# Up tiles of the experts in transfers of 2 MB, and transposes of the identity on TensorE while the experts' places are worked out

## The reference

```python
def moe_ffn(h, router_w, w1, w3, w2):
    logits = (h @ router_w).astype(jnp.float32)
    top_vals, top_idx = lax.top_k(logits, TOP_K)
    ...
    for e in range(N_EXPERTS):
        out = out + gate[..., e:e + 1].astype(h.dtype) * swiglu(h, w1[e], w3[e], w2[e])
    return out

def swiglu(h, w1, w3, w2):
    return (jax.nn.silu(h @ w1) * (h @ w3)) @ w2
```

## Time and profile before

| | |
|---|---|
| median of 3 executions | 2174.63 us (2174.55 to 2176.81) |
| the profiled execution | 2175.69 us, its span 2173.9 us |
| TensorE busy | 2070.3 us (95%) |
| VectorE busy | 1270.5 us (58%) |
| ScalarE busy | 946.6 us (44%) |
| read from HBM | 485.91 MB |
| DMA queue of SyncE | 484.39 MB |

### The profile page before, as it was taken

How to read it: one execution, slowest core, us unless ns; L and a number is a source line. 1 busy time by engine, 2 the same in 40 slices (tenths; PEclk the granted TensorE clock), 3 DMA queues, 4 the chain that set the end, 5 groups by cost and what they waited for, 6 DMA issues and landing times. The chain is left out here.

```text
span 2173.9 us, 38831 instructions
## 1 busy us (share of the span) xinstructions
PE 2070.3 (95%) x15492; PEld 1737.7 (80%) x15492; DVE 1270.5 (58%) x2412; ACT 946.6 (44%) x1724; POOL 124.9 (6%) x115
## 2 busy tenths in 40 slices
PE   8999999999999999998999899998999999999997
PEld 7988888998978988888999888888556765568553
DVE  5465667565667776778665775777114931178211
ACT  5545544545554453446443544444014630065111
POOL 0100000010000024021000005012000000000000
PEclk9999999999999999999999999999999999999999
DMA  6443334444337444346554444339999999999997
GB/s 198 151 136 101 98 98 140 145 144 136 113 123 163 142 152 131 106 137 219 172 191 137 138 147 145 107 118 346 392 421 420 421 413 420 420 421 407 409 420 310
DMA packets 257818, 489.49 MB, mean 225 GB/s; under 512 B 35256, under 2 KB 208216, under 8 KB 223720
## 3 DMA queue, kind: packets, MB, share of 16 engines
q1 hardware_dynamic: 252112, 484.39, 61.6%
q0 software_dynamic: 656, 1.80, 0.2%
q10 hardware_dynamic: 4872, 0.81, 0.2%
HBM read 485.91 MB, written 1.05 MB: 224 GB/s over the span
## 5 line engine op out<-in xcount | busy, mean ns | idle before, releaser
L1356 PE MATMUL bank<-memr 128*128 128x256 f32 (+3 forms) x7056 | 896.6, 286 | 28.4 <-DVE memr L2417 9.7
L1356 PEld LDWEIGHTS bank<-memr 128*128 128x128 f32 (+2 forms) x7056 | 855.5, 185 | 58.8 <-issue 16.3
L2417 DVE TENSOR_TENSOR memr<-mem_low,memr 128x1024 fp32r<-128x1024 f32 (+3 forms) x328 | 400.0, 1238 | 63.8 <-ACT memr L1864 63.1
L1864 ACT CAST memr<-mem_low 128x1024 fp32r<-128x1024 f32 (+3 forms) x328 | 333.3, 1032 | 112.7 <-PE bank L1356 109.8
L1252 DVE SCALAR_TENSOR_TENSOR mem_high<-mem_high,bank 128x128 f32<-128x128 f32 (+1 forms) x88 | 28.0, 318 | 273.4 <-ACT mem_high L1053 273.4
L1053 ACT ACTIVATE mem_high<-bank 128x128 f32<-128x128 f32 (+1 forms) x88 | 26.7, 304 | 348.1 <-PE bank L869 322.8
L869 PE MATMUL bank<-mem_tail,mem_low 128*64 128x256 f32 x1088 | 127.5, 387 | 2.9 <-DMA mem_tail<-in_moe 2.3
L869 PEld LDWEIGHTS bank<-mem_tail,mem_low 128*64 128x64 f32 x1088 | 77.9, 139 | 54.2 <-issue 17.3
L660 PE MATMUL bank<-memr 128*128 128x256 f32 x960 | 115.6, 281 | 3.1 <-DVE memr L2436 3.1
L869 PE MATMUL bank<-mem_ring,mem_low 128*64 128x256 f32 x992 | 113.7, 381 | 3.7 <-DMA mem_ring<-in_moe 3.7
L660 PEld LDWEIGHTS bank<-memr 128*128 128x128 f32 x960 | 114.3, 189 | 3.5 <-issue 3.5
(11 more groups left out here) (367 smaller groups left out, 2815.6 us busy)
## 6 DMA issues: line engine op xcount, KB each, us to landing
mem_tail<-in_moe SPq DMA_DIRECT2D x132, 1024.0 KB, 15.4
mem_ring<-in_moe SPq DMA_DIRECT2D x128, 1024.0 KB, 16.2
mem_low<-in_w_in SPq DMA_DIRECT2D x112, 1024.0 KB, 5.2
mem_tail<-in_ffn_w SPq DMA_DIRECT2D x18, 1024.0 KB, 8.6
mem_low<-in_w_out SPq DMA_DIRECT2D x16, 1024.0 KB, 5.3
mem_low<-in_w_branch SPq DMA_DIRECT2D x12, 1024.0 KB, 5.0
mem_high<-in_ffn_w SPq DMA_DIRECT2D x12, 1024.0 KB, 8.1
mem_low<-in_w_branch SPq DMA_DIRECT2D x16, 512.0 KB, 3.5
```

What stands on the lines that cost most here:

```text
L1356: ins = pe.matmul(out(bank), lhsT, rhs, start=((k, i) == order[0] and not half), stop=((k, i) == order[-1]), skip_group_check=half is not ...
L1864: cp(high, raw).then_inc(*sig("w_high", i))
L2417: st(V.tensor_tensor(low, raw, high, ALU.subtract), sig("w_split", i))
```

## The change

Each chunk's two up tiles become one tile of 2 MB: the weights lie in memory so that a partition's 4096 numbers are contiguous, and one transfer brings them (128 rows of 16 KB in place of 128 rows of 8 KB twice). Of the twelve places eight become four pairs, used by up tiles alone, and four stay single, used by down tiles alone. Of the four places that are free after `chosen`, three and the fourth make room for the pairs of chunks 4 and 5; the second of these is still two transfers. A pair is asked for when both halves of the chunk four before it are finished, a down tile when the down tile four before it is. `LOAD_ORDER` keeps the order of use, but puts the pairs of chunks 4 and 5 after the tiles that can be loaded before `chosen`. On TensorE `keep_clock` transposes the identity matrix 12 times into the bank of the places before the wait for `chosen`, and 8 times into the bank `XB` behind the counts of places.

```diff
+PAIRS = 4
+RAW = 3 * PAIRS
+LOAD_ORDER = [n for n in range(TILES) if TILE_ORDER[n][1] != 1]
+LOAD_ORDER.sort(key=lambda n: (FIRST if PAIRS <= TILE_ORDER[n][0] < PAIRS + HI // 2 and TILE_ORDER[n][1] == 0 else n, n))
...
+        def pair_of(g):
+
+            return g if g < PAIRS + HI // 2 else (g - PAIRS - HI // 2) % PAIRS
...
+            def keep_clock(bank, n):
+
+                for _ in range(n):
+                    pe.transpose(bank[:, 0:P], const("ident"), const("ident"))
...
             ins.then_inc(*sig("token_sums", 0))
             tokens(1)
+            bank = open_group(("place",))
+            keep_clock(bank, 12)
 
             pe.wait_ge(*at("chosen"))
             pe.sem_inc(family("m_done"), HI)
...
             ins.then_inc(*sig(f"acc_full{unit['place',] % 2}", "place"))
+            keep_clock(XB, 8)
             pe.wait_ge(*evacuated("place"))
...
-                for n in range(TILES):
+                for n in LOAD_ORDER:
...
-                    if n < FIRST:
-                        sp.wait_ge(family("m_done"), p * (TILES + FIRST) + n + 1)
+                    k = pair_of(g)
+                    if j == 2 and g >= PAIRS:
+                        sp.wait_ge(*tile_done(p, down_tile(g - PAIRS)))
+                    elif j < 2 and g >= PAIRS + HI // 2:
+                        sp.wait_ge(*tile_done(p, up_tile(max(q for q in range(g) if pair_of(q) == k), 1)))
                     else:
-                        sp.wait_ge(*tile_done(p, n - (FIRST if n < FIRST + RAW else RAW)))
-                    src = a["moe"][bass.DynSlice(expert[i], 1), c, j].rearrange("o p f -> (o p) f") if i else a["moe"][0, c, j]
-                    sp.dma_start(raw[slot_of(n)], src).then_inc(raw_loaded(p, n)[0], 16)
+                        sp.wait_ge(family("m_done"), p * (TILES + FIRST) + (FIRST if j < 2 and k >= PAIRS else RAW))
+                    if j == 2:
+                        sp.dma_start(single[g % PAIRS], weights(expert, i, c, 2)).then_inc(raw_loaded(p, n)[0], 16)
+                    elif k > PAIRS:
+                        for half in range(2):
+                            sp.dma_start(last_raw[half], weights(expert, i, c, 0)[:, 2048 * half:2048 * (half + 1)])\
+                                .then_inc(raw_loaded(p, n)[0], 16)
+                    else:
+                        sp.dma_start(wide_hi[:, 0:4096] if k == PAIRS else pair[k], weights(expert, i, c, 0))\
+                            .then_inc(raw_loaded(p, n)[0], 16)
```

More of the change, by code:

```diff
@@ L44 @@
 W2B = 384
-RAW = 12
+PAIRS = 4
+RAW = 3 * PAIRS
 HI = 4
@@ L315, in build @@
         top[0] = upper
-        raw, raw_r = map(list, zip(*[carve_both(2048) for _ in range(6)]))
+        pair, pair_r = map(list, zip(*[carve_both(4096) for _ in range(3)]))
         top[0] = mark
-        for i in range(5):
-            raw.append(mem_ring[:, 2048 * i:2048 * (i + 1)])
-            raw_r.append(carve_both(2048)[1])
+        pair.append(mem_ring[:, 0:4096])
+        pair_r.append(carve_both(4096)[1])
+        single, single_r = [], []
+        for i in range(2, 5):
+            single.append(mem_ring[:, 2048 * i:2048 * (i + 1)])
+            single_r.append(carve_both(2048)[1])
         htok = [carve(D)]
@@ L758, in heavy_before, with raw_tile, raw_tile_r @@
             return sum(heavy(k) for k in range(i))
-        def slot_of(n):
-            return n if n < FIRST else (n - FIRST) % RAW
-        def raw_loaded(p, n):
[L766 to L772, removed]
+        def pair_of(g):
+            return g if g < PAIRS + HI // 2 else (g - PAIRS - HI // 2) % PAIRS
+        def raw_tile(n, singles=single, pairs=pair, rest=(wide_hi[:, 0:4096], last_raw)):
+            g, j = TILE_ORDER[n]
+            if j == 2:
+                return singles[g % PAIRS]
+            k = pair_of(g)
+            if k > PAIRS:
+                return rest[1][j]
+            return (rest[0] if k == PAIRS else pairs[k])[:, 2048 * j:2048 * (j + 1)]
+        def raw_tile_r(n):
+            return raw_tile(n, single_r, pair_r)
+        def raw_loaded(p, n):
+            g, j = TILE_ORDER[n]
+            if j == 2:
+                return family(f"m_down{g % PAIRS}"), 16 * (p * UPS // PAIRS + g // PAIRS + 1)
+            k = pair_of(g)
+            if k >= PAIRS:
+                last = max(range(k - PAIRS, len(chunks), NSLOT))
+                s, before = at(f"w_loaded{k - PAIRS}", last)
+                return s, before + 16 * (k - PAIRS + 1) * (p + 1)
+            of_place = [q for q in range(UPS) if pair_of(q) == k]
+            return family(f"m_up{k}"), 16 * (p * len(of_place) + of_place.index(g) + 1)
         def split_done(p, n):
@@ L857, in up @@
                         pe.wait_ge(*split_done(p, n))
-                        high, low = hi_r[SPLIT.index(n) % HI], raw_r[slot_of(n)]
+                        high, low = hi_r[SPLIT.index(n) % HI], raw_tile_r(n)
                         for k in range(4):
@@ L977, in moe_sync, with weights @@
         def moe_sync(sp):
+            def weights(expert, i, c, j):
+                lo, f = (0, 4096) if j < 2 else (P * 4096, 2048)
+                if i == 0:
+                    return a["moe"][0, c, lo:lo + P * f].rearrange("(p f) -> p f", f=f)
+                return a["moe"][bass.DynSlice(expert[i], 1), c, lo:lo + P * f].rearrange("o (p f) -> (o p) f", f=f)
             def body(p, learn):
                 expert = {0: 0}
-                for n in range(TILES):
+                for n in LOAD_ORDER:
                     g, j = TILE_ORDER[n]
```

33 lines of the change are left out of this document (17 added, 16 removed).

## The result

| | before | after |
|---|---|---|
| median, taken in turns on one chip | 2175.34 us (8 runs, 2172.32 to 2179.02) | 2182.88 us (8 runs, 2180.89 to 2187.78) |
| the profiled execution, its span | 2175.69, 2173.9 | 2183.04, 2181.1 |
| first transfer of the stage to its last landing | 672.9 | 679.3 |

The changed kernel is slower: the ratio is 1.0037, with a 95% interval of 1.0026 to 1.0047. Of the 7.2 us between the two spans the stage itself (first issue of `in_moe` to the last landing) has 6.4.

The account below looks back on a forecast made before the run. DMA at 420 GB/s was taken to bound light experts, TensorE heavy ones. Losses in the opening and at both heavy experts, less saved packets, summed to +7.6 us on the profiled 2175.69; median 2182, range 2174 to 2189.

Parts of the forecast that it names:

- Packets: Experts' stage: each pair loaded by one transfer saves 71 ns; 4.1 us (58 pairs) reach the end.
- 16 KB rows give nothing but marks: Rival, whole stage: 58 pairs lose 63 ns each of the saving, 3.7 us more, 2185.9 us; chance 0.1.
- the saving arrives whole: Rival, heavy stretches: the queue is not starved there, so the sum is -5.0 us, 2169.6; chance 0.1.
- Transposes: Before and through the gather: the 20 transposes hold TensorE's clock at 2.4 GHz, costing TensorE about 0.1 us.
- second rival: Opening: the transposes do not hold the clock, the sum is +13.1 us, 2187.7; chance 0.12.
- Opening: Start of the stage: a wait in SyncE's order loses 5.1 us where 3.9 was lost before, +1.2.
- First heavy start: First heavy expert: waiting for both halves puts its start at +2.1 us; a clock fall costs 2.5, TensorE leaves at +4.6.
- Second heavy start: Second heavy expert: its first chunk waits for a whole pair (+2.5 us), so TensorE starts at +7.0.
- The ends of the heavy experts: Low transfer rates there lose 7 to 8 us at each, where 0.5 and 2.6 were lost before.
- late asking: Heavy ends: a pair is asked for only when its second half is free; 1.2 us at the first, 1.8 at the second.
- the wait for a whole pair: Both heavy starts: both halves must have landed before work begins, 2.5 us later at each.
- The clock: First heavy expert: after a longer idle time TensorE's clock falls to 0.50, charged 2.5 us; no new price at the second.

Follow-up runs that it names:

- e: The changed kernel with each pair except chunk 4's brought by two 1 MB transfers, asked for together and counted on one semaphore; 2184.27 us.
- a: The changed kernel without its 20 transposes of the identity; 2186.52 us.
- c: The changed kernel with the pairs of chunks 7 and 8 ahead of the down tiles of chunks 4 and 5 in SyncE's order; 2180.62 us.
- f: The changed kernel with each pair except chunk 4's as two transfers asked for together, each half with its own semaphore; 2181.66 us.
- i: As f, but each half is asked for as soon as TensorE has finished the same half of the chunk before it in that place; 2176.94 us.
- g: The changed kernel with only the first pair of each heavy expert brought by two transfers, each with its own semaphore; 2180.19 us.
- d38: The changed kernel with 38 transposes of the identity ahead of the first up of each heavy expert; 2179.64 us.
- h: The changed kernel with the edits of c and g, and 24 transposes before the first up of each heavy expert; 2178.47 us.
- b: The kernel before with the 20 transposes of the opening alone, tiles still of 1 MB; 2173.11 us.

## Why the prediction was right, step by step

The forecast was 2182.0 us and slower; the median is 2182.88. The direction and the places of the loss were right; that the sum fits so well is in part luck, since its terms were off in opposite directions.

- **Packets**, 71 ns a pair: right. A pair lands each 4.89 us, full stretches run at 424 to 425 GB/s, and e, with the old packets, at 420. But of the 4.1 us that were to reach the end, e shows 2.7 by the stage and 1.4 by the medians. The rivals "16 KB rows give nothing but marks" and "the saving arrives whole" fall by the same rows: full stretches are faster, and both heavy ends did starve.
- **Transposes**: right that the clock stays, at 1.00 from 1512 to 1530, judged by a row that held the same kind of work. The Trainium skill (TensorE: Matmul & The Clock Gate, Part 4) says that a transpose does not count as work for the gate. Here the changed kernel with and without 20 of them shows the opposite (1.00 against 0.60). `up(0)` started at 1522.7, 1.2 us later than worked out: VectorE's tables now ended at 1521.9 and its copy at 1522.6, since `chosen` itself came 0.8 later in this execution. The second rival's time, 2187.7, stands beside 2186.52 for a, in which the clock does fall.
- **Opening**: 5.1 us lost was forecast and 5.0 measured, at the place named, with other pieces, so the fit is luck. The price of an empty queue was misread: the transfer issued at 1528.02 took 6.7 us, but the one before it landed only at 1529.9 (1515.79 + 14.1), so the queue was not empty, and it landed 4.8 behind that one. Into a queue that was empty (0 GB/s from 1535 to 1537) the down tile landed in 4.7 us. In exchange it was asked for 1.5 us behind the last landing, where 0.9 was worked out, and the pair right behind it came 1.3 later than a full queue would bring it. Chunk 9 landed 1.6 us later than before (75.4 against 73.8), forecast +1.2, and chunk 22 then 0.5 earlier, forecast 0.4 earlier.
- **First heavy start**: +2.1 forecast, +1.9 measured against the first issue of the stage (175.9 against 173.9), the idle time 4.8 and not 3.9, the first up 8.48 (+2.6, forecast +2.5). The fit of the first up is partly luck: behind the same idle time of 4.8 us it took 8.48 in the changed kernel, 8.61 in a and 7.39 in c, so the price of a fall changes from one run to the next. TensorE left the expert +3.6 and not +4.6: from the first up to the end of the last one it needed 90.2 us where the kernel before needed 91.2. DMA stood at +4.9 (chunk 40), forecast +5.8.
- **Second heavy start**: +6.1 measured, +7.0 forecast; DMA behind it +7.9 (chunk 71), forecast +8.8; the last landing +6.4, forecast +7.6. The ends of the heavy experts lost 6.4 and 7.6 us of landings, forecast 7 to 8 each.
- **The mis-sized term** is the late asking, "1.8 later. Before, the queue ran out only at the very end (0.5 lost), so I take 1.2 of it", and 1.8 at the second. f against i measures 3.0 and 3.3 us. I priced one ask, the last, but each pair asked for late at a heavy end adds to the last, as long as the queue is empty: in the changed kernel the pairs of chunks 35, 36 and 37 land 3.6, 1.2 and 1.2 us later than full stretches would bring them, those of chunks 68, 69 and 70 3.6, 1.4 and 1.8. On the other side, the wait for a whole pair was charged 2.5 twice, while g shows 2.7 to 4.4 for both starts. The clock was charged 2.5 once, at the first heavy expert; d38 shows 3.1 for the falls at both, of which the second stood in the kernel before too. And h shows that the two overlap, while the forecast added them up. The sum came out because these errors fill each other.

The account of the stage along one chain of kernels, from before to after: transposes -2.0 (before to b), order and places by kind +2.4 (b to i), late asking +6.0 (i to f), packets against waiting for a whole pair 0.0 (f to after; by e it is -2.7 for the packets and +2.7 for the wait). Together 6.4, which is the difference between before and after by the way it is counted. By the medians it is -2.9, +3.8, +4.7 and +1.2: 6.8 of the 7.5. Each stage is one execution, and the two counts differ by up to 1.4 us in a term, which is how well a term is known.

## What to carry to other kernels

A larger transfer saves its packets in every stretch (here 0.07 of 5 us, 1.4%), but it is asked for when its last half is free and usable when its last half has landed; where TensorE, which reads the tiles, is behind and the queue runs empty, that cost more here than the packets saved. Before fusing transfers, look for stretches in which the rate falls below its full value: there the moment of asking decides. A wait of TensorE can be filled with transposes of a constant into an idle bank; filled to its end it cost nothing here and the work behind ran at 2.4 and not 1.2 GHz, filled for 3.0 of 4.8 us it moved the fall behind the wait (first ups of 7.4 us, against 5.8 with no fall).

## What had not been expected of the hardware

- A transfer of 1 MB into an empty queue took 4.7 us to land (issue 1536.57; 4.8 for the first of the stage in the kernel before), and a pair 7.7 (the first of the changed kernel), where a full queue brings a tile each 2.5 us. The 6.7 of the earlier trace rows held 1.9 us of the transfer before it. A time to landing is the price of an idle start only if the landing before it came ahead of the issue.
- In a the clock fell within an idle time of 1.61 us ahead of the products of 8 columns, behind turns of the tokens and products of few columns (these ten products then took 2.27 us, not 1.25). At the first heavy start of the kernel before, an idle time of 1.78 us, behind the down of a light chunk and a few short products, left it at 1.00 (first up 5.86 us). So the length of the gap alone did not decide. What TensorE had done before it differs between the two; that this is the reason is not shown.
- Equal waits had unequal prices: behind an idle time of 3.8 to 3.9 us the first up of a heavy expert took 7.26 and 8.62 us in b, 8.49 and 7.41 in i.
- With two transfers and one semaphore (e) in place of one transfer the stage grew by 2.7 us, and by 1.4 in the medians, less than the 4.1 that the packet price gives for 58 pairs.
